# Attention reciprocals applied at other ticks, gates' low halves four ticks later, and four warm-up matmuls instead of two in a two-layer hybrid decoder on one Trainium2 core

## The reference

```python
def hybrid_layer(h, ...):                       # h: 528 rows that count (16 meta + 512) x 2048
    proj = rms_norm(h, norm_g) @ w_in
    qa, fa, ia, ga, qb, kb, vb, gb, uc, gc = jnp.split(proj, splits, axis=-1)
    ya = rms_norm(hgrn2_mixer(qa, fa, ia, lb, valid), hgrn_norm_g)      # 4 heads of 128
    yb = swa_sink_attention(qh, kh, vh, sinks)                          # 16 heads of 64, window 128
    yc = multiscale_pool(uc, valid, pool_w, pool_scale)
    mixed = jnp.concatenate([ya * silu(ga), yb * silu(gb), yc * silu(gc)], axis=-1)
    return h + mixed @ w_out

# inside swa_sink_attention
    denom = jnp.sum(pr, axis=-1, keepdims=True) + jnp.exp(sink - mx)
    o = einsum(pr / denom, v_all)
```

## Time and profile before

| | |
|---|---|
| median of 3 runs | 1561.88 us |
| fastest and slowest of them | 1560.76 and 1562.08 us |
| the profiled execution: its own time | 1559.15 us |
| its span, from the first instruction to the last | 1557.3 us |
| TensorE busy | 1540.7 us |
| VectorE, ScalarE, GpSimd busy | 947.4, 646.9 and 196.9 us |

### The profile page before, as it was taken

The page is one execution under the profiler, slowest core; times in us unless marked ns, Lnnn a source line. Parts: engine busy times, 40 slices in busy tenths (PEclk is TensorE's granted clock), DMA queues, the critical chain, the costliest instruction groups (busy, mean ns, idle before and its releaser), DMA issues.

```text
span 1557.3 us, 26363 instructions
## 1 busy us (share of the span) xinstructions
PE 1540.7 (99%) x10456; PEld 1423.1 (91%) x10456; DVE 947.4 (61%) x1829; ACT 646.9 (42%) x1291; POOL 196.9 (13%) x348
## 2 busy tenths in 40 slices
PE   8999999999999999999999999999999999999999
PEld 8999899999999999999998889888999878888888
DVE  6787687777678445334335776876787774442322
ACT  6776566622332323232235665666232342321211
POOL 0112664400000000000000006544000000000000
DMA  7222112122221223344342222112223122234442
GB/s 279 99 82 82 56 55 72 65 71 95 83 72 65 82 93 112 124 135 153 124 136 100 81 85 79 55 60 77 83 82 109 55 82 95 95 123 149 136 150 68
DMA packets 39307, 151.78 MB, mean 97 GB/s; under 512 B 5376, under 2 KB 14352, under 8 KB 24336
## 3 DMA queue, kind: packets, MB, share of 16 engines
q1 hardware_dynamic: 38752, 149.52, 28.7%
q10 hardware_dynamic: 432, 0.57, 0.1%
HBM read 141.22 MB, written 8.59 MB: 96 GB/s over the span
## 4 chain that ended last, share of the span: by engine, by line
PE 89%; DVE 4%; DMA 2%; SPq 1%; POOL 1%; issue 1%; ACT 1%; DVEq 0%; POOLq 0%; ACTq 0%
PE ps_gemm L1142 77%; PE ps_mix L1029 2%; PE ps_mix L948 2%; PE ps_mix L994 2%; PE ps_mix L962 2%; PE ps_gemm L909 1%; DMA x_in<-in_xT 1%; DMA a_rden<-rden 1%; PE ps_gemm L1103 1%; PE ps_gemm L896 1%; SPq L461 1%; PE ps_mix L896 1%; SPq L465 1%; PE ps_mix L990 1%; DVE w_lo L1214 1%
## 5 line engine op out<-in xcount | busy, mean ns | idle before, releaser
L1142 PE MATMUL ps_gemm<-x_hi,w_hi 128*128 128x264 f32 (+3 forms) x2176 | 542.2, 314 | 0.5 <-issue 0.5
L1142 PE MATMUL ps_gemm<-x_hi,w_lo 128*128 128x264 f32 (+3 forms) x2176 | 528.1, 307 | 0.0
L1142 PE MATMUL ps_gemm<-x_lo,w_hi 128*128 128x264 f32 (+3 forms) x2176 | 527.6, 307 | 0.0
L1142 PEld LDWEIGHTS ps_gemm<-x_hi,w_hi 128*128 128x128 f32 x2176 | 353.6, 189 | 20.0 <-issue 0.9
L1142 PEld LDWEIGHTS ps_gemm<-x_hi,w_lo 128*128 128x128 f32 x2176 | 352.1, 188 | 19.4
L1142 PEld LDWEIGHTS ps_gemm<-x_lo,w_hi 128*128 128x128 f32 x2176 | 351.5, 188 | 16.9
L645 ACT ACTIVATE w_hi<-w_stage 128x512 fp32r<-128x512 f32 x464 | 267.0, 618 | 169.5 <-DVE z L1307 122.7
L1214 DVE TENSOR_TENSOR w_lo<-w_stage,w_hi 128x512 fp32r<-128x512 f32 x392 | 256.8, 690 | 66.2 <-ACT w_hi L645 60.4
L1142 PE MATMUL ps_gemm<-mixed_hi,w_lo 128*128 128x264 f32 (+1 forms) x752 | 199.0, 320 | 0.0
L1142 PE MATMUL ps_gemm<-mixed_lo,w_hi 128*128 128x264 f32 (+1 forms) x752 | 198.7, 319 | 0.0
L1142 PE MATMUL ps_gemm<-mixed_hi,w_hi 128*128 128x264 f32 (+1 forms) x752 | 197.6, 318 | 0.0
(11 more groups left out here) (195 smaller groups left out, 1626.9 us busy)
## 6 DMA issues: line engine op xcount, KB each, us to landing
w_stage<-in_w_in SPq DMA_DIRECT2D x82, 1024.0 KB, 4.9
w_stage<-in_w_out SPq DMA_DIRECT2D x32, 1024.0 KB, 5.3
res<-in_xT SPq DMA_DIRECT2D x16, 264.0 KB, 5.3
h1T<-z SPq DMA_DIRECT2D x16, 264.0 KB, 5.7
res<-h1T SPq DMA_DIRECT2D x16, 264.0 KB, 5.3
a_rden<-rden SPq DMA_DIRECT2D x32, 128.0 KB, 4.9
out<-z SPq DMA_DIRECT2D x15, 256.0 KB, 5.6
x_in<-in_xT SPq DMA_DIRECT2D x2, 1056.0 KB, 13.7
```

Source lines behind the costliest of these rows:

```text
L1142: ins = pe.matmul(g[:, bank, 0:size], ws, xs[:, k, c:c + size], start=tick == 0 and i == 0, stop=tick == TICKS - 1 and i == 2)
```

## The change

Three things change, and one constant gets a name. Eight products with reciprocals and the second set of reciprocal loads go to other places; the low halves of the gates go from tick 5 to tick 9, in all 16 gate slots of each layer; and the warm-up has four matmuls.

```diff
+GATE_LOW_TICK = 9
...
-WARM_MATMULS = 2
+WARM_MATMULS = 4
...
-RECIP_LOAD_SLOTS = (22, 26)
-RECIP_AT = ((23, 0), (23, 9), (23, 11), (25, 10), (26, 11), (28, 10), (28, 14), (29, 0))
+RECIP_LOAD_SLOTS = (22, 27)
+RECIP_AT = ((23, 9), (23, 11), (25, 10), (26, 9), (28, 10), (28, 14), (29, 9), (29, 11))
...
-                    if tick == 5 and pkind == "gate":
+                    if tick == GATE_LOW_TICK and pkind == "gate":
                         gate_low(N - 1)
```

## The result

The changed kernel takes 1553.91 us (median of 4 runs, 1553.74 to 1554.62), the kernel before 1561.98 us beside it (4 runs, 1560.76 to 1566.98). The medians are 8.1 us apart. The ratio is 0.9945, with an interval of 0.9928 to 0.9961: 0.55% faster, 0.39 to 0.72%.

A forecast was written before the change was run, and what follows sets the result against it. The prediction took TensorE's queue as the bound, with only its 16.6 us not busy and modelled ends to gain; 1.61 + 0.97 + 1.55 + 0.3 = 4.4 us off 1561.9 gave 1557.5 us, range 1554.5 to 1561.3 us.

The forecast's parts named there:

- The first product, 1.6 us: Slot 23, first layer: moving the product from (23, 0) to (23, 9) ends a TensorE stall, gaining 1.6 us.
- the fifth product, 2.5 us: Slot 27, first layer: moving the product from (26, 11) to (28, 10) ends two TensorE stalls, gaining 2.5 us.
- The median of the runs is 2.7 us above that execution; I take the same 4.4 us off it: Last step of the sum: the profiled execution's 4.4 us gain applied unchanged to the median, 1561.9 to 1557.5 us.
- rival D: Loads reach (28, 10) too late, so the wait only moves: 2.5 us of gain lost, 1560.0 us, chance 0.04.
- "Nothing" for the second layer: Second layer's reciprocals: only the third wait, 3.4 us on VectorE, falls; TensorE shows no stall by it, so no gain.
- The gates in slot 31, 0.3 us: Slot 31: moving the gates' low halves shortens TensorE's wait for h_k by 0.15 us per layer, 0.3 us together.
- "Nothing" for the attention: Slots 15 to 18: moved low halves gain nothing; bounds 0.5 us gained and 8 times 0.7 us lost.
- rival A: Attention: low halves meet GpSimd's products and slow down, 1563.7 us; chance 0.09 in full, 0.09 in part (1560.6).
- mixed_lo at 0.7 us, not 1.7: Sign to look for in slots 15 to 18: mixed_lo takes 0.7 us, with no new TensorE wait behind a_pt_lo.
- The warm-up: Kernel start: two more warm-up matmuls gain nothing and lose at most 1.2 us; taken as nothing.
- B: Slots 24, 27 or 30: h_qp late again, 1 to 3 us of the gain returned, 1559.5 us, chance 0.12.
- C: Slot 31 gives its full 1.5 us and the attention 0.5 us: 1555.8 us, chance 0.12.

The follow-up runs named there:

- e9_again: The changed kernel measured once more, nothing altered, for a comparison on one chip: 1553.94 us, ratio 0.9947.
- e2_recips: The kernel before with only the new places of the reciprocals' products and their loads: 1554.96 us, ratio 0.9962.
- e1_warm: The kernel before with four warm-up matmuls instead of two and nothing else: 1561.54 us, ratio 0.9998.
- e3_gates: The kernel before with only the gates' low halves moved from tick 5 to tick 9: 1561.42 us, ratio 1.0001.
- e6_second: The kernel before with only the second wait for reciprocals removed, its loads moved to slot 27: 1558.71 us, ratio 0.9975.
- e5_first: The kernel before with only the first wait for reciprocals removed, the second set's loads left in slot 26: 1559.77 us, ratio 0.9987.
- e10_gate5: The changed kernel with the gates' low halves back at tick 5: 1554.92 us, ratio 0.9953.
- e11_wlow: The changed kernel with slot 31's second low part of weights made at tick 7, behind the updates of h_k: 1552.79 us, ratio 0.9941.
- e4_after_warm2: The changed kernel with two warm-up matmuls instead of four: 1554.52 us, ratio 0.9957.
- e12_stall12: The changed kernel with twelve unused VectorE products added at the start of slot 23, first layer: 1561.12 us, ratio 0.9993.

## Why the prediction was wrong, point by point

**What bounds the kernel.** Right: all of the gain is idle time of TensorE, at the places named.

**The first product, 1.6 us; the fifth product, 2.5 us.** The mechanism was right, and so were both sizes for that one execution: the stalls are gone. That the spans differ by just the sum is luck. The gates brought 0.95 us where 0.3 was taken, and the changed kernel's execution was 0.69 us later at the end of its start (20.58 against 19.89), where 0 was taken; the two errors nearly cancel. In e9_again, the same kernel with no late start (19.83), the span is 1552.1 us, 5.2 less than before. The step that failed is the last one of the sum, "The median of the runs is 2.7 us above that execution; I take the same 4.4 us off it". These 2.7 us were taken as something that the change leaves alone. They were part of what it removes. e2_recips, with this part alone, gained 7.5 us by its median (5.9 by its ratio) where these two terms had 4.1, and the runs that had lain 4.1 us apart lay 0.9 us apart. Three things stand in the place of that step.

- The waits for the loads differ between executions of kernels that are the same in these slots: 5.04 to 6.51 us for the first, 5.89 to 6.87 us for the second, and behind a fixed cover TensorE pays the difference in full. The profile that the terms were read from had the shortest of both.
- Behind the longer stalls of slot 23 TensorE ran at half clock for a time, which cost 1.5 us in each of the traces of e1_warm, e3_gates and e6_second. The profiled execution of before had none of it. In how many runs of before the clock fell is not known. Of the 60 beside the experiments 47 have a mean clock below 1.000, with a median of 1562.69 us, and that of the other 13 is 1560.37. But 3 us at half clock are only 0.001 of the mean, the quickest of the 60 and two of the five runs of e2_recips show 0.999 too, and runs with the fall can have had the longer stalls as well.
- The trace of e1_warm shows what a run near the median loses. Its own time of 1562.54 us is near the 1562.2 us that is the median of those 60. Its stalls of 3.11, 1.04 and 1.54 us and the 1.5 us of half clock are 7.2 us, and with the 1.0 us of the gates 8.2. From that execution the change would have been worth what the medians show, 8.1 us; from the profiled one it was 4.5.

The profiled execution's time lay 2.7 us under the median and 1.6 us under the quickest of the three runs shown. That was in the forecast's own table, and was the sign that this execution might stand for a short case.

**The loads in slot 27 (rival D).** Right, with a last issue 2 us later than worked out and no wait. D fell. "Nothing" for the second layer was right for the profiled execution; e5_first's trace shows that a wait there of 4.32 us, 0.9 us longer, stops TensorE for 0.72 us.

**The gates in slot 31, 0.3 us.** Right at the place: 0.26 and 0.23 us where 0.2 us was read from ScalarE's row, and 1.5 us were refused. With all 16 slots, the move is worth 1.0 us (e10_gate5). The rest lies in the attention, at two places: 0.27 us in slot 18 of the first layer and 0.19 in slot 16 of the second. There `mixed_lo` stood ahead of an `a_pt_lo` and TensorE came 0.2 to 0.3 us too early. All six traces with the low halves at tick 5 have both stalls (0.62 to 0.63 and 0.67 to 0.70 us), and all eight with tick 9 have neither (0.36 and 0.48 us). "Nothing" for the attention was thus 0.5 us too low, at its bound; its step "No stall of TensorE in these slots of either layer ends at a `mixed_lo`" was read from modelled idle times, which hide these two. That the `w_lo` behind is what holds `h_k` is shown by e11_wlow: with it out of the way, the 0.5 us left in each layer go.

**The attention and GpSimd (rival A).** The mechanism is there, the loss is not. Of the eight `mixed_lo` in slots 15 to 18 of both layers four took 1.13 to 1.29 us, among them the one shown above, 0.44 to 0.6 us more than the 0.69 to 0.71 of the others, all started during a product of GpSimd. Step "mixed_lo at 0.7 us, not 1.7" was thus half wrong. But it was paid from idle time, as the text had it: VectorE's waits for `a_pt_hi` there went from 3.6 us to 1.3 us, and no wait of TensorE came. At the one place where TensorE had paid for such a meeting, that of the earlier trace rows, the `mixed_lo` of the changed kernel took 0.69 us (at 1020.16). Rival A's rule holds in these rows and costs nothing here.

**The warm-up.** Nothing that can be told, as taken: e1_warm's ratio is 0.9998. In the changed kernel's trace the products run at full pace almost at once, and TensorE gives it back in waits for `x_lo` (0.78 us twice). The group of the earlier trace rows that started at 19.89 us started at 20.58 in the changed kernel and at 19.83 in e9_again, at 20.39 with two matmuls (e4_after_warm2). Two executions of the same kernel differ by 0.75 us here, so it is not the warm-up that sets it; that it is the arrival of the inputs is argued from the waits for `x_lo`.

**Rivals B and C.** In the changed kernel no stall came back in slots 24, 27 or 30, and the pair of products in slot 29 costs nothing that the waits show; B fell. C (1555.8 us) had the right side for the wrong reason: it looked for 2.0 us in slot 31 and the attention, where the gates' move gave 1.0; the reciprocals gave 3.4 us more than their terms by the medians. No rival asked whether the profiled execution stands for the median one, and so the range ended too high.

What stays open: by the medians e5_first and e6_second together gain 5.6 us and both edits at once 7.5 us; by the ratios it is 5.9 us both times, so this gap may be no more than the error of the medians. In e5_first, without the first wait, four of 11 runs still have a mean clock of 0.998 and 1561.1 us or more: a fall of the clock behind another wait would fit, but its one trace shows none. And what makes one load land later in one execution than in another was not found.

## What to carry to other kernels

Before a sum is made from one profile, set that execution's own time against the runs: if it is quicker than all of them, the waits in it may be the shortest ones, as here, and a change that removes a wait for memory gains the waits of the median run, with what follows them. A spread of several us in a kernel can be such a wait; here it went from 4.1 to 0.9 us with the wait. Price a stall of a busy TensorE with the clock behind it: where the granted clock fell here, 1.5 to 2.4 us came on top, and removing what one execution showed as 1.6 and 2.5 us was worth 5.9 to 7.5. And look for small stalls in the starts of matmuls, not in idle times: two of 0.2 to 0.3 us stood in no list of waits.

## What the runs showed of the hardware that was not expected

- The granted clock went to half behind stalls of 2.01, 2.62, 3.11, 3.31 and 4.80 us, each in the trace of one execution, and stayed at 1.00 behind stalls of 1.61 and 1.81 us, and behind one of 1.91 us in slot 27 (e3_gates). It is not the same in each run of one kernel: with 10 extra products 7 of 10 runs show the lower mean clock, with 12 all 11. What decides it in a run was not found.
- The fall has no fixed place against the end of the stall. In e1_warm the clock was still 0.98 on average from 364 to 366 us, while TensorE was back at work from 364.85, and 0.50 in the next 3 us. In e12_stall12 it was 0.50 from 365 to 366 us, and TensorE came back at 366.30.
- The same loads at the same place of the program kept VectorE 5.04 us in one trace and 6.51 us in another, and the kernel before, unchanged, spread over 2.9 to 6.0 us in its runs. In the first set it is the last of 16 loads that lands later: issued at 351.52 in before and waited for until 359.29 (7.8 us), in e1_warm issued at 351.78 and waited for until 361.04 (9.3 us). In the second set it is the issuing: in e3_gates, with one issue of 1.40 us instead of 0.61, the last started 11.1 us after the first (402.98 to 414.08), in before 10.2 (401.15 to 411.32), and VectorE went on 4.7 to 4.8 us after the last in both. Why was not found.
- A product of VectorE with two inputs that starts during a product of GpSimd took up to 0.6 us longer in the changed kernel (1.29 instead of 0.71 us), and 1.0 us longer in one place of the kernel before (1.66 instead of 0.69).
